# A mixture-of-experts decoder block: the list of overfull experts made two experts earlier

## What is computed

```
logits = tok @ w_router + b_router
vals, idx = top_k(logits, 4);  wts = softmax(vals)
gates = the four weights of a token at its experts, 0 elsewhere
for each expert e:
    hgu   = tok @ w_gate_up[e] + b_gate_up[e]            # 1024 -> 2048
    x_glu = min(hgu[:, 0::2], 7);  x_lin = clip(hgu[:, 1::2], -7, 7)
    act   = x_glu * sigmoid(1.702 * x_glu) * (x_lin + 1)
    acc  += gates[:, e] * (act @ w_down[e] + b_down[e])  # 1024 -> 1024
h = rms_norm(h + acc, g_final)
```

## Time and profile before

| what | value |
|---|---|
| median of three runs | 1006.41 us |
| lowest and highest | 1006.39 and 1010.56 us |
| the profiled execution's own time | 1006.83 us |
| its span in the trace | 1005.0 us |
| PE, busy share of the span | 97% |
| DVE, ACT, POOL | 23%, 16%, 5% |
| bytes moved by DMA | 418.90 MB |
| granted TensorE clock | 0.999 |

### The profile page before, as it was taken

The page is one execution under the profiler, slowest core; times in us unless marked ns, Lnnn a source line. Parts: engine busy times, 40 slices in busy tenths (PEclk is TensorE's granted clock), DMA queues, the critical chain, the costliest instruction groups (busy, mean ns, idle before and its releaser), DMA issues.

```text
span 1005.0 us, 11664 instructions
## 1 busy us (share of the span) xinstructions
PE 976.6 (97%) x4737; PEld 387.7 (39%) x4737; DVE 235.8 (23%) x624; ACT 163.0 (16%) x312; POOL 45.4 (5%) x89
## 2 busy tenths in 40 slices
PE   9999999999999999999999999999999999999996
PEld 7888433333343333333333333333333333333332
DVE  6986311112211111111111111111111111111121
ACT  5783211111101000111111101110011110100112
POOL 2860000000000000000000000000000000000000
PEclk9999999999999999999999999999999999999999
DMA  9999999999999999999999999999999999999995
GB/s 272 361 398 425 363 407 425 428 429 432 435 431 429 431 432 430 430 434 430 430 434 433 430 430 436 428 430 437 430 430 434 429 430 434 425 428 428 427 424 239
DMA packets 36802, 418.90 MB, mean 417 GB/s; under 512 B 5915, under 2 KB 16427, under 8 KB 19494
## 3 DMA queue, kind: packets, MB, share of 16 engines
q1 hardware_dynamic: 36038, 418.17, 98.9%
q10 hardware_dynamic: 736, 0.34, 0.1%
HBM read 417.45 MB, written 1.05 MB: 416 GB/s over the span
## 4 chain that ended last, share of the span: by engine, by line
PE 82%; DMA 14%; ACT 2%; another core or an unknown queue 1%; DVE 0%; issue 0%; SPq 0%; ACTq 0%; DVEq 0%
PE bank L1487 37%; PE bank L1532 19%; DMA gu_ring<-in_w_gate_up 10%; PE bank L1285 6%; PE bank L1459 5%; PE bank L1397 4%; DMA dn_ring<-in_w_down 4%; PE bank L1304 3%; PE bank L1391 3%; ACT reg L750 2%; PE bank L1508 1%; PE bank L1502 1%; PE bank L1224 0%; SPq L396 0%
## 5 line engine op out<-in xcount | busy, mean ns | idle before, releaser
L1487 PE MATMUL bank<-gu_ring,reg 128*64 128x512 f32 x2048 | 450.4, 595 | 11.1 <-DMA gu_ring<-in_w_gate_up 11.0
L1487 PEld LDWEIGHTS bank<-gu_ring,reg 128*64 128x64 f32 x2048 | 142.6, 137 | 310.1 <-issue 285.3
L1532 PE MATMUL bank<-dn_ring,reg 128*64 128x512 f32 x1024 | 227.4, 595 | 7.7 <-ACT reg L750 7.2
L1114 DVE TENSOR_SCALAR reg<-bank 128x256 f32<-128x256 f32 x64 | 24.2, 420 | 587.4 <-PE bank L1487 587.4
L1532 PEld LDWEIGHTS bank<-dn_ring,reg 128*64 128x64 f32 x1024 | 70.5, 137 | 143.0 <-issue 124.5
L745 ACT ACTIVATE reg<-reg 128x512 f32<-128x512 f32 x29 | 18.3, 630 | 456.4 <-DVE reg L1114 456.4
L1459 PE MATMUL bank<-reg 64*128 64x512 f32 x256 | 63.9, 616 | 0.9 <-DVE reg L1183 0.9
L1285 PE MATMUL bank<-dn_ring,gu_ring 128*128 128x272 f32 (+1 forms) x256 | 59.0, 390 | 0.3 <-ACT reg L612 0.3
L1397 PE MATMUL bank<-xh,reg 128*64 128x512 f32 x248 | 58.5, 592 | 0.0
L1285 PEld LDWEIGHTS bank<-dn_ring,gu_ring 128*128 128x128 f32 x256 | 48.4, 190 | 9.6 <-DMA gu_ring<-in_w_in 0.6
L752 ACT ACTIVATE reg<-bank 128x512 f32<-128x512 f32 x29 | 17.3, 597 | 208.4 <-PE bank L1532 208.4
(11 more groups left out here) (257 smaller groups left out, 424.7 us busy)
## 6 DMA issues: line engine op xcount, KB each, us to landing
gu_ring<-in_w_gate_up SPq DMA_DIRECT2D x46, 4096.0 KB, 33.0
dn_ring<-in_w_down SPq DMA_DIRECT2D x22, 4096.0 KB, 33.0
gu_ring<-in_w_gate_up SPq DMA_DIRECT2D x31, 2048.0 KB, 39.2
dn_ring<-in_w_down SPq DMA_DIRECT2D x10, 2048.0 KB, 20.3
dn_ring<-in_w_down SPq DMA_DIRECT2D x17, 1024.0 KB, 14.2
gu_ring<-in_w_gate_up SPq DMA_DIRECT2D x9, 1024.0 KB, 7.8
gu_ring<-in_w_in SPq DMA_DIRECT2D x6, 1024.0 KB, 12.3
dn_ring<-in_w_out SPq DMA_DIRECT2D x4, 1024.0 KB, 11.2
```

Source lines behind the costliest of these rows:

```text
L1114: ins = V.tensor_scalar(half(xglu, b), glu_v[:, 0], 7.0, None, ALU.min)
L1487: ins = mm(gub[b][64 * h:64 * h + 64, :], xgT[:, j, :], of_half(gu_ring[:, s, j, 1024 * b:1024 * b + 1024], h), start=False, stop=(j == KD ...
L1532: ins = mm(out[64 * h:64 * h + 64, :], a[:, at:at + SLOTS], dn_ring[:, s, k, 512 * h:512 * h + 512], start=(i == 0), stop=(i == KD - 1))
```

## The change

The constant `LIST`, which sets the pair of experts at which the list is made, goes from 2 to 1. The hook of expert 4 moves to expert 2, that of 5 to 3, of 6 to 4, and of 7 to 5. DVE's loop of one iteration goes away. Experts 6 and 7 have no hook any more and become the first iteration of the loops of PE and of DVE. SP's and ACT's programs are the same as before. No arithmetic is added or taken away.

```diff
--- before.py
+++ after.py
@@ -32,7 +32,7 @@
 
 XCOLS = 16
 ITEMS = NE + XCOLS
-LIST = 2
+LIST = 1
 SP_EXP, SP_DONE = 3, 24
 NEG_EPS, LN_EPS = 1e-6, 1e-5
 
@@ -1144,9 +1144,6 @@
 
             expert(0, 1, 4, between=over_64, split=True)
             expert(1, 0, 4)
-            with v.Fori(1, LIST) as g:
-                two_experts(g)
-
             def list_copies():
 
                 v.wait_ge(x_pe, 3)
@@ -1619,22 +1616,20 @@
             def wait_gain():
                 pe.wait_ge(x_dve, 4)
 
-            def two_experts(g, first=None, then=None):
-                expert(g * 2, 1, g - 2, g * 2 - 1, {0: (dw_in[1], (g - 2) * 16)}, halves=True, **(first or {}))
-                expert(g * 2 + 1, 0, g - 1, g * 2, {0: (dw_in[0], (g - 2) * 16)}, halves=True, **(then or {}))
+            def two_experts(g):
+                expert(g * 2, 1, g - 2, g * 2 - 1, {0: (dw_in[1], (g - 2) * 16)}, halves=True)
+                expert(g * 2 + 1, 0, g - 1, g * 2, {0: (dw_in[0], (g - 2) * 16)}, halves=True)
 
             def quarters(s, counts):
                 return {2 * j: (dq_in[s][j], n * 16) for j, n in enumerate(counts) if n}
 
             expert(0, 1, 1, None, quarters(1, (1, 0, 1, 1)), freed=PK, rows_out=True, down_with=dict(order=(0, 4, 1, 5, 2, 6, 3, 7), used=(0, 1, 5), hooks={4: second_turned}), hooks={0: second_part, 1: gather_rest, 2: turn_rest, 4: all_places, 6: counts})
             expert(1, 0, 1, 0, quarters(0, (1, 0, 1, 1)), freed=PK, first_used=True, down_with=dict(used=(1, 5)))
-            expert(2, 1, 2, 1, quarters(1, (3, 1, 2, 2)), freed=PK, rows_in=True)
-            expert(3, 0, 2, 2, quarters(0, (2, 1, 2, 2)), row_0=(row3_in, 16))
             mid = KD // 2
-            expert(4, 1, 3, 3, dn_halves(1, 1), hooks={mid: list_places})
-            expert(5, 0, 1, 4, dn_halves(0, 1), halves=True, hooks={mid: list_counts}, before_turn=wait_list)
-            two_experts(LIST + 1, dict(hooks={mid: list_tables}, before_turn=wait_tables),
-                        dict(hooks={mid: gain_rows}, before_turn=wait_gain))
+            expert(2, 1, 2, 1, quarters(1, (3, 1, 2, 2)), freed=PK, rows_in=True, hooks={mid: list_places})
+            expert(3, 0, 2, 2, quarters(0, (2, 1, 2, 2)), row_0=(row3_in, 16), hooks={mid: list_counts}, before_turn=wait_list)
+            expert(4, 1, 3, 3, dn_halves(1, 1), hooks={mid: list_tables}, before_turn=wait_tables)
+            expert(5, 0, 1, 4, dn_halves(0, 1), halves=True, hooks={mid: gain_rows}, before_turn=wait_gain)
             with pe.Fori(LIST + 2, NE // 2 - 2) as g:
                 two_experts(g)
             expert(NE - 4, 1, 4, NE - 5, dn_halves(1, 2))
```

## The result

The changed kernel took **1008.75 us** (median of 22 runs, 1006.62 to 1011.50), the kernel before 1006.89 us (22 runs beside it; one of them took 4251.99 us, which does not move the median). The ratio is 1.0017 with an interval of 1.0010 to 1.0024: 1.7 us slower by the ratio (1.9 us by the medians), and clear of zero, though within the 0.5% that I had called no change. The time is inside the range of 1005.2 to 1009.5 us. The forecast of 1006.4 us, no movement, was wrong.

What follows compares the result with a forecast made beforehand. The DMA stream was taken to bound the kernel, so PE's moved work, waits and loops each added 0 to the profiled 1006.83 us; the median lying 0.42 us lower gave 1006.4 us, range 1005.2 to 1009.5 us.

Steps and rivals of the forecast that it cites:

- What bounds the kernel: From 217 us on at the latest the DMA stream bounds; PE time counts only if its queue runs dry.
- cover: Time from a load's issue to the landing of the transfer ahead of it; 3.4 us forecast at the tightest issues.
- PE's hooks and its lateness: Experts 2 to 7 on PE: 7.71 us of hooks only moved; PE 5.38 us late after expert 4, 5.63 after 5.
- How much cover is enough: Short queues early in the trace gave needs of 2.1 or 3.1 us; 3.4 us suffices, loss 0, upper bound 1.4.
- the two tight loads: Down loads of experts 6 and 7, issues forecast at 250.0 and 279.2 us, 3.4 us before the landing ahead.
- The hooks' waits: PE's hooks waiting on ACT's and DVE's copies: 0 us, at most 1.42 us in the stretch of counts.
- The loops: One more turn of PE's loop and DVE's lost branch: 0 us.
- The rivals: Queue running dry, stall at PE's loop (both slower), small gain of 0.5 us (0.04), or PE setting the end (sum 0).
- The dry queue: At experts 6 and 7's down loads, 1 us per us beyond cover, up to 5.6; with a stall, over 5 us: 0.03.
- partial case: Part of PE's lateness lost at the down loads of experts 6 and 7: 1 to 4 us, 1007.4 to 1010.4; chance 0.06.
- signs given for a wrong forecast: DMA share under 0.95 at 240 to 285 us, landings there moved over 1 us, or PE waiting for DVE at a gather.

Runs made afterwards that it cites:

- fullrow_e12: Kernel before with 9 useless matmuls over all 128 rows (7.9 us) added at expert 12: 1007.69 us against 1007.06.
- bias_gain_67: Changed kernel with the down bias moved to expert 6 and the gain to expert 7, both straight code: 1007.12 us against 1006.96 before.
- fullrow_short_e3: Kernel before with 5 useless matmuls over all 128 rows (4.5 us) added at expert 3: 1008.78 us against 1006.64.
- fullrow_e3: Kernel before with 9 useless matmuls over all 128 rows (7.9 us) added at expert 3: 1012.80 us against 1007.06.
- straight67: Changed kernel with experts 6 and 7 put back into straight code on PE: 1009.85 us against 1006.96 before.

## Why the prediction was wrong

- **What bounds the kernel** was right. The DMA stream sets the end: lateness well within the cover is free (fullrow_e12, bias_gain_67), beyond it it counts one for one (fullrow_short_e3, fullrow_e3).
- **PE's hooks and its lateness** were right: 27.40, 28.92, 29.18, 27.11 and 27.12 us, and where the clock held (straight67) SP's issues came at 250.4 and 279.6 us, for 250.0 and 279.2 forecast. The covers there were 3.6 us both times, for 3.4.
- **"How much cover is enough"** is the step that failed. I read a need of 2.1 and 3.1 us from two places at the beginning of the program, where the pieces in the queue were 1 MB and smaller, and took a loss of 0, since both rows agreed. The runs show that 3.4 us was not enough: at 3.1 to 4.0 us of cover 5 of 11 loads landed late, and with 3.6 us one of the two tight loads of straight67 did, by 1.5 us. The term that I set to 0 measured 1.1 to 1.4 us where the clock held. Three things were wrong with the reading. Each row was a single event. The margin over the need of 3.1 us was 0.3 us, while the cover of one and the same load differs by 0.7 us between the two profiles of before (7.4 and 6.7 us). And the DMA share of a window does not show a load that lands late: in straight67 it is 0.99 to 1.02 in the four windows of 5 us from 275 to 295 us. The landing distances do show it. With the need of about 5 us that the fillers' medians give, the forecast's own numbers would have given a loss of some 1.6 us: 1008.0 us.
- **A smaller slip.** The working says that the two loads after expert 7's move by 2.1 us at most, and under the rivals that expert 8's first half moves by 5.63 us to a cover of 5.1 us. The second is right. In straight67 that load, issued at 287.7 us, had 6.7 us and landed on time, so nothing hung on it.
- **The clock** was missing from the sum. I took 30.70 us for the tables' expert as a constant. It is 32.34 us where the clock falls, and this is worth most where the cover is gone.
- **The hooks' waits**: no wait of PE on DVE appeared; 0 us, right.
- **The loops**: 27.11 and 27.12 us for experts 6 and 7, 0 us on PE, right. The changed kernel even fetches 18 blocks of code in place of 20. That the fetches take part in the DMA stream I had not seen; it works for the change, by an estimated 0.4 us at the rate above.
- **The rivals.** The dry queue was the right mechanism, with its place and its price of 1 us for each us beyond the cover, and it had too small a chance because of the wrong need. Its partial case, 1007.4 to 1010.4 us at 0.06, is what came. Two of the signs given for a wrong forecast came with it: in the changed kernel's profile a window with a share of 0.65 (250 to 255 us), and a landing of expert 6's down weights at 264.5 us in place of 263.1. That 1008.75 us lies inside the range is owed to the room left for a partial loss and for scatter, not to the sum.

## What to carry to other kernels

When the DMA engines set the end, ask of every edit on another engine how late it makes the next issue, and compare that with the cover that a trace shows there; measure the need of cover with a filler of known length at that place before trusting a margin of a few tenths of a us. Judge a load by its landing less the landing ahead, not by the DMA share of a window, and look whether a fetch of code fell into it. A load that frees half its buffer early, and is issued in two parts there, buys cover cheaply; done everywhere, the extra DMAs cost more than they bring. Work that a full queue hides is best put where the queue is long, and as little of it as possible at once.

## What was not expected of the hardware

- A run of 32-row matmuls, back to back, pulled TensorE's granted clock to 0.50, the lower level (17 of them took 26 us), while 9 matmuls over 128 rows (7.9 us) left it at 1.00.
- Loads of 4 MB issued 3.1 to 4.0 us before the landing of the load ahead landed late in 5 of 11 cases, by up to 1.5 us; with under 3 us always (8 of 8), with more than 4 us hardly ever (3 of 850 where no fetch of code fell in).
- Code is not free in a full DMA queue: about 0.2 us for each fetch of 16 KB (an estimate from three medians), and about 0.05 us for each further DMA when 4 MB come as two.
- What brings the clock down in the hook of the tables in both profiles of the changed kernel, and what lowers the mean clock in 11 of its 33 runs, stays open.
